# A hybrid decoder block on one core: the input projection as seven products of halves

## The reference, cut to what matters

```
D_MODEL = 2048; SEQ = 512; N_META = 16
POOL_WIDTH = 1024; DN_WIDTH = 2048; DN_HEADS = 16; DN_HEAD_DIM = 128
IN_SPLIT_SIZES = (1024, 1024, 2048, 2048, 2048, 2048, 16, 16, 2048, 2048)

def hybrid_layer(h, ...):                       # h: (1, 528, 2048) float32
    xn = rmsnorm(h, norm_w)
    proj = xn @ w_in                            # (528, 2048) @ (2048, 14368)
    u_pool, z_pool, q, k, v, z_dn, b, a, gate_pool, gate_dn = split(proj)
    y_pool = causal_multiscale_pool(u_pool, pool_mix, pool_scale) * silu(z_pool)
    y_dn = gated_deltanet_branch(q, k, v, z_dn, b, a, ...)   # conv of 4 taps, silu,
                                                # chunked delta rule, 16 heads
    merged = sigmoid(gate_pool) * (y_pool @ w_pool_out) + sigmoid(gate_dn) * (y_dn @ w_dn_out)
    return h + merged @ w_o                     # then a final rmsnorm, meta tokens dropped
```

## Time and profile before

| | us |
|---|---|
| three runs | 1962.67, 1962.79, 1963.48 (median 1962.79) |
| span of the profiled execution | 1960.8 |
| PE busy | 1931.4 (99%) |
| PEld busy | 1724.3 (88%) |
| DVE busy | 921.4 (47%) |
| ACT busy | 726.0 (37%) |
| POOL busy | 78.3 (4%) |
| DMA, mean over the span | 115 GB/s |

### The profile page before, as it was taken

The page is one execution under the profiler, slowest core; times in us unless marked ns, Lnnn a source line. Parts: engine busy times, 40 slices in busy tenths (PEclk is TensorE's granted clock), DMA queues, the critical chain, the costliest instruction groups (busy, mean ns, idle before and its releaser), DMA issues.

```text
span 1960.8 us, 35753 instructions
## 1 busy us (share of the span) xinstructions
PE 1931.4 (99%) x13729; PEld 1724.3 (88%) x13729; DVE 921.4 (47%) x2315; ACT 726.0 (37%) x2136; POOL 78.3 (4%) x105
## 2 busy tenths in 40 slices
PE   5999999999999999999999999999999999999998
PEld 5888899999999999999999988888888888888886
DVE  6333343656556466555646654322224444335332
ACT  5422223435353443535345353323234322224232
POOL 4000000000000000000000000000000000000000
PEclk8999999999999999999999999999999999999999
DMA  6133342433333242333334144333443534347302
GB/s 222 59 103 102 102 134 88 119 95 86 95 120 90 87 124 69 96 111 100 91 107 123 44 131 127 119 107 128 134 162 134 186 118 139 118 139 279 108 22 86
DMA packets 221302, 225.73 MB, mean 115 GB/s; under 512 B 33665, under 2 KB 197978, under 8 KB 220522
## 3 DMA queue, kind: packets, MB, share of 16 engines
q1 hardware_dynamic: 158898, 180.17, 28.1%
q10 hardware_dynamic: 55944, 22.63, 4.6%
q0 software_dynamic: 6336, 21.08, 3.4%
HBM read 199.65 MB, written 25.30 MB: 115 GB/s over the span
## 4 chain that ended last, share of the span: by engine, by line
PE 97%; ACT 1%; DVE 1%; issue 0%; POOL 0%; DMA 0%; ACTq 0%; SPq 0%; DVEq 0%
PE pj L530 82%; PE pg L530 10%; PE pt L530 3%; PE pt L679 1%; PE pg L781 0%; POOL xl L1696 0%; DVE fst L1233 0%; ACT xsquare L908 0%; DMA xt<-in_meta_tokens 0%; PE pj L574 0%; DVE xl L1239 0%; ACT wh L868 0%; DVE xt L1246 0%; ACT L1041 0%; ACT L1070 0%
## 5 line engine op out<-in xcount | busy, mean ns | idle before, releaser
L530 PE MATMUL pj<-xh,wh 128*128 128x512 f32 (+3 forms) x2688 | 735.1, 328 | 3.2 <-DVE wl L1208 3.1
L530 PE MATMUL pj<-xh,wl 128*128 128x512 f32 (+3 forms) x2688 | 712.4, 319 | 0.0
L530 PE MATMUL pj<-xl,wh 128*128 128x512 f32 (+3 forms) x2688 | 712.3, 319 | 0.0
L1208 DVE TENSOR_TENSOR wl<-raw,wh 128x256 fp32r<-128x256 f32 x896 | 344.2, 421 | 603.0 <-ACT wh L868 601.5
L530 PEld LDWEIGHTS pj<-xh,wh 128*128 128x128 f32 x2688 | 446.9, 189 | 43.2 <-DVE wl L1208 3.4
L530 PEld LDWEIGHTS pj<-xh,wl 128*128 128x128 f32 x2688 | 448.4, 188 | 35.9
L530 PEld LDWEIGHTS pj<-xl,wh 128*128 128x128 f32 x2688 | 448.8, 189 | 33.9 <-issue 1.0
L868 ACT ACTIVATE wh<-raw 128x256 fp32r<-128x256 f32 x896 | 307.0, 410 | 64.7 <-issue 45.0
L868 ACT ACTIVATE wh<-rawb 128x256 fp32r<-128x256 f32 (+1 forms) x224 | 85.0, 437 | 217.0 <-PE pj L530 189.8
L530 PE MATMUL pj<-yl,wh 128*128 128x512 f32 x384 | 149.5, 389 | 0.0
L530 PE MATMUL pj<-yh,wl 128*128 128x512 f32 x384 | 149.5, 389 | 0.0
(11 more groups left out here) (243 smaller groups left out, 1784.3 us busy)
## 6 DMA issues: line engine op xcount, KB each, us to landing
raw<-in_w_in SPq DMA_DIRECT2D x112, 1024.0 KB, 6.2
rawb<-in_w_dn_out SPq DMA_DIRECT2D x16, 1024.0 KB, 6.3
rawb<-in_w_o SPq DMA_DIRECT2D x12, 1024.0 KB, 5.3
gates_scratch<-stg ACTq DMA_DIRECT2D x32, 256.0 KB, 2.1
rawb<-in_w_pool_out SPq DMA_DIRECT2D x8, 1024.0 KB, 5.7
gst<-gates_scratch POOLq DMA_DIRECT2D x32, 256.0 KB, 3.1
yraw<-branch_scratch SPq DMA_DIRECT2D x1, 5632.0 KB, 23.1
xt<-in_x SPq DMA_DIRECT2D x4, 1024.0 KB, 6.2
```

Of the source, the lines that this page charges most:

```text
L530: return pe.matmul(dst, lhs, rhs, start=start, stop=stop)
L1208: tt(wl[:, j, 2 * q:2 * q + 2, :], raw[:, 2 * par + h, 2 * q:2 * q + 2, c * P:(c + 1) * P], wh[:, j, 2 * q:2 * q + 2, :].bitcast(F32), ALU ...
```

## The change

The 256 columns and 2048 rows of a block are taken as four quarters of 1024 rows by 128 columns, A and C (upper rows), B and F (lower rows), and the positions as two halves of 264 (eight meta tokens and 256 positions each). The four half-size results are got from seven products instead of eight, each of 1024 rows by 128 columns by one half of positions: sums and differences of quarters and of input halves go in, and sums of products come out. A product is two chunks of four weight tiles. The order in a block is `(1, 4, 6, 2, 5, NEXT, 3)`, where NEXT is product 7 of the following block.

- PE: 7 x 8 x 3 = 168 matmuls of 264 columns a block (q: 260; z, z_pool and gate: 256) in place of 96 of 512 or 192 of 256 to 272. Products 4, 6, 5, NEXT and 3 wait for a copy or an addition of the block.
- ACT: 14 high-part copies of 512 elements instead of 16 of 256, and three copies of a bank into `snap` a block; one of the four results is copied out by `last_to_time` or squashed in two parts.
- DVE: 14 subtractions of 512 elements instead of 16 of 256; four weight sums of 1024 elements (`s1` to `s4`); three combinations of a bank with a snapshot (`c11`, `c21`, `c22`).
- SP: one transfer of 1 MB for A and C together with 1 KB runs, and one of 512 KB with 512 B runs for each of B and F, into five quarter buffers that are written over in place; SP's loads are written out in an order of their own, with the reloads of k, q, v and z among them.
- The weight buffers hold four chunks (`RINGS`), split three chunks ahead of PE (`AHEAD`).
- To make room, k, q, v and z of a pair go through a scratch tensor in HBM (`head_scratch`): ACT stores each head after its SiLU, SP reloads them one pair later. `zst` and `vch` now lie in `tm`, so POOL waits for the store of a pair before it loads the row sums of the next.
- At the start the five input combinations and their parts are made (ten halves of 1056 elements each for sums and for low parts, most on DVE), some before the first product and some within block 0. The small product for beta and decay moves from pool group 0 to group 1.
- The delta steps are spread over 112 half-chunk hooks (`delta_step`), with step m at hook 15m/8.

```diff
+NEXT = 0
+ORDER_FIRST = (1, 2, 7, 6, 4, 5, NEXT, 3)
+ORDER = (1, 4, 6, 2, 5, NEXT, 3)
+ORDER_LAST = (1, 4, 6, 2, 5, 3)
+AHEAD = 3
+RINGS = 4
...
+            def block_loads(b, col, between=None):
+
+                order, base = order_of(b), base_of(b)
+                sp.wait_ge(lo_done, base + after(order, 1))
+                sp.wait_ge(sum_done, 4 * b + 3)
+                load_ac(col)
+                if between == "v":
+                    load_vch(between_pair[0])
+                sp.wait_ge(lo_done, base + after(order, 5))
+                load_raw(RF, col)
+                if between == "kq":
+                    load_kq(between_pair[0])
+                if between == "z":
+                    load_zst(between_pair[0])
+                sp.wait_ge(lo_done, base + after(order, 3))
+                load_raw(RB, col)
...
+        def delta_step(h):
+
+            return next((m for m in range(O0 + 6) if 15 * m // 8 == h), None)
...
-                    for w, xx, first, last in ((wh, xh, True, False), (wh, xl, False, False), (wl, xh, False, True)):
-                        for dst, c0, n in halves:
-                            mm = product(dst, w[:, slot, k, :], xx[:, kt, c0:c0 + n],
-                                         first and kt == 0, last and kt == KT - 1)
...
+                for i, what in enumerate(order):
+                    if what == 1:
+                        need(pe, last_done, b - 1)
+                    elif what == 2:
+                        need(pe, add_done, 3 * b)
+                    elif what == 4:
+                        pe.wait_ge(snap_done, snapped(b, "s4"))
+                    elif what == 6:
+                        pe.wait_ge(snap_done, snapped(b, "s1"))
+                    elif what == 5:
+                        pe.wait_ge(snap_done, snapped(b, "s2"))
+                    elif what == 3:
+                        pe.wait_ge(add_done, added(b, "C22"))
+                    elif what == NEXT:
+                        pe.wait_ge(add_done, added(b, "C21"))
...
+                        pe.wait_ge(lo_done, base + chunk + 1)
+                        for k in range(HK):
+                            kt = HK * h + k
+                            for w, xx, one, last in ((wh, xh, True, False), (wh, xl, False, False), (wl, xh, False, True)):
+                                mm = pe.matmul(bank[:, c0:TH], w[:, slot, k, :], xx[what][:, kt, c0:TH],
+                                               start=opens and one and kt == 0, stop=closes and last and kt == KH - 1,
+                                               skip_group_check=True)
...
+                of, what, half, chunk, slot = split_target(b, par, t)
+                dve.wait_ge(hi_done, chunk + 1)
+                tt(wl[:, slot, :, :], weights(SLOT_OF[what])[:, HK * half:HK * (half + 1), :], wh[:, slot, :, :].bitcast(F32),
+                   ALU.subtract).then_inc(lo_done, 1)
...
+                for t in range(2 * len(order)):
+                    if t == (3 if first else 0):
+                        s2(b)
+                    if t == (7 if first else 1):
+                        s1(b)
+                    if t == (8 if first else 5):
+                        s4(b)
+                    if not last and t == (9 if first else 6):
+                        s3(b + 1)
+                    split_lo(b, par, t)
+                    if t == (10 if first else 7):
+                        free(1)
+                        c21(b, kind, dst[1])
+                    if t == (12 if first else 10):
+                        c22(b, par, kind, dst[1])
+                    event(t)
+                    if t == (13 if kind in ("k", "q", "v") or first else 12 if kind == "u" else 11):
+                        free(0)
+                        c11(b, kind, dst[0])
+                    hook(2 * t)
+                    hook(2 * t + 1)
...
+            row_differences(0)
+            with pool.Fori(1, PAIRS) as d:
+                head_out(d - 1)
+                pool.wait_ge(y_stored, 16 * d)
+                row_differences(d)
+            head_out(PAIRS - 1)
```

More of the change, by code:

```diff
@@ L74, with base_of, order_of, after @@
 NGATE = 2 * D // CW
-CB = 512
-NCB = D // CB
 NCP = CP_GATE0 + NGATE
+SLOT_OF = {1: 0, 2: 2, 3: 2, 4: 3, 5: 3, 6: 4, 7: 4, NEXT: 4}
+RA, RC, RB, RF, RE = range(5)
+def base_of(b):
+    return 0 if isinstance(b, int) and b == 0 else 14 * b + 2
+ALL_CHUNKS = base_of(NCP - 1) + 2 * len(ORDER_LAST)
+def order_of(b):
+    if isinstance(b, int):
+        return ORDER_FIRST if b == 0 else ORDER_LAST if b == NCP - 1 else ORDER
+    return ORDER
+def after(order, product):
+    return 2 * order.index(product) + 2
 CI = 0
@@ new lines, in gate_block, with event, last_pair, before @@
+            def gate_block(i, par, before, hook):
+                def event(t):
+                    before(t)
+                    ends = 2 * len(order_of(CP_GATE0 + i))
+                    if t == ends - 2:
+                        second_squashed(CP_GATE0 + i, stg[:, 1, :], ACT.Sigmoid, gate_sig)
+                    if t == ends - 1:
+                        gate_store(i, 1)
+                block_acts(CP_GATE0 + i, par, "gate", "gate", event, hook)
+            for k in range(4):
+                def last_pair(h, k=k):
+                    m = delta_step(28 * k + h)
+                    if m is not None:
+                        delta(PAIRS - 1, m)
+                def before(t, k=k):
+                    if k == 0:
+                        z_tail(PAIRS - 1, t)
+                    else:
+                        gate_tail(k - 1, 1 - k % 2, t)
+                gate_block(k, k % 2, before, last_pair)
@@ new lines, in block_steps @@
+            def block_steps(b, par, kind, dst, free, event, hook):
+                order = order_of(b)
+                first, last = 7 in order, NEXT not in order
+                for t in range(2 * len(order)):
+                    if t == (3 if first else 0):
[12 more added lines that the diff above has]
+                        c22(b, par, kind, dst[1])
+                    event(t)
+                    if t == (13 if kind in ("k", "q", "v") or first else 12 if kind == "u" else 11):
+                        free(0)
+                        c11(b, kind, dst[0])
+                    hook(2 * t)
+                    hook(2 * t + 1)
@@ new lines, in x_lo_part @@
+            def x_lo_part(what, half, source, high):
+                rows = slice(HK * half, HK * (half + 1))
+                dve.wait_ge(x_hi, high)
+                tt(xl[what][:, rows, :], source[:, rows, :], xh[what][:, rows, :].bitcast(F32), ALU.subtract).then_inc(x_lo, 1)
+            dve.wait_ge(x_f, 17)
+            for half in range(2):
+                x_total(fd, f12, f22, ALU.subtract, half)
+            split_lo(0, 0, -3)
+            s3(0)
+            split_lo(0, 0, -2)
+            for half in range(2):
+                x_lo_part(7, half, fd, 5 + half)
+                dve.wait_ge(x_sum, 1 + half)
+                dve.wait_ge(x_lo, 1 + half)
+                x_total(fd, fd, f11, ALU.subtract, half)
@@ new lines, in free, with hook @@
+                    def free(c, k=k):
+                        if k == 3:
+                            dve.wait_ge(head_stored[c], 16 * (4 * p + 3))
+                        else:
+                            need(dve, conv_step, (6 * p + 2 * k + 1 - c) * 4)
+                    def hook(h, k=k):
+                        m = delta_step(28 * k + h)
+                        if d is not None and m is not None:
+                            delta(d, m)
+                    dst = [xin[:, TAPS - 1:]] * 2 if k < 3 else [stg[:, c, :] for c in range(2)]
```

1045 lines of the change are left out of this document (652 added, 393 removed).

## The result

The changed kernel takes 2038.18 us (median of four runs, 2030.75 to 2041.82), the kernel before 1962.75: a ratio of 1.038, 95% interval 1.036 to 1.040. Predicted were 1890 us and a gain of 73; it came out 75 us slower, on the side to which I had given 0.08. The profiled execution has a span of 2035.1 us.

A forecast was written before the change was run, and what follows sets the result against it. PE bound the kernel before; after, DVE in k and q, PE in v and z. Gains 12 (pool stage), 10 (pair 0), 19 (seven pairs), 7 and 25 (gate blocks) make 73: 1962.8 - 73, about 1890 us, range 1842 to 1932.

The forecast's parts named there:

- PE's part: Projection matmuls: a u, k or v block wins 3.1 us, q 2.8, the others 2.2; a pair wins 11.2.
- DVE's part: DVE's work per block goes from 5.4 to 14.1 us; a pair has 102.7 us of DVE against 104.7 of PE.
- the sum by blocks: In a pair, the larger of DVE and PE per block: k 27.4, q 25.6, v 34.5, z 20.5, together 108 us.
- Waits that the change adds: In a pair, waits between engines and for `dec`: 4 us for k and q, 1 for v, making 113 us.
- the clock: PE's clock should stay at 1.00 (2.4 GHz); if waits push it lower, the forecast is too low; no size given.
- The chain for `dec`: On POOL: y's store, row sums, then `dec`, 13.9 us in all; DVE waits 1.5 us for it in block k.
- The start: Block 0 ends near 67 us, with 36 us of DVE work from about 31 us on; it loses 6 us.
- The end: Passage from the gate blocks to stage B: 1 us taken off the 26.4 us won by twelve gate blocks.
- the fourth: Rival: delta-step rounds between PE and DVE cost twice the waits, P 128.7, 2000 us, deciding from P = 123.4; chance 0.08.
- P: Length of a pair with a delta rule: 115.7 us before, forecast 113, forecast's own range 109 to 117.
- The formula: Whole kernel's time as 1962.8 - 54 - 7 x (115.7 - P), with P the length of a pair.

The follow-up runs named there:

- e5: e4 with the row sums loaded into `dec` itself before y is stored, and v's reload waiting for that store: 1973.7 us.
- e4: Changed kernel with the pair loop written out, k and q reloaded eight chunks earlier, and the `yraw` load cut into five pieces: 1987.2 us.
- e1: Changed kernel with the loop over pairs 1 to 7 written out on PE, ACT and DVE: 2032.6 us.
- e6: e5 with the loop over the pairs kept on PE, ACT and DVE: 2015.0 us.
- e3: Changed kernel with the 5 MB `yraw` load cut into five pieces issued between earlier weight loads: 2023.9 us.
- e7: e5 with DVE's four weight sums cut to an eighth in every block but the first, output not the reference's: 1909.1 us.
- e12: e5 with 12 and 5 filler matmuls on PE ahead of two waits in the inverse of block v: 1971.1 us.
- e11: e5 with nine of the fourteen steps of the block inverse left out on DVE, output not the reference's: 1949.6 us.
- e8: e5 with the two rounds that turn and square q moved ahead of the block inverse: 1995.5 us.

## Why the prediction was wrong

**PE's part** was right where nothing interferes. The gate stores come every 19.88 us, so a matmul of 256 columns starts every 118.3 ns instead of the 117 taken; the timeline of the changed kernel, gate blocks 6 to 8:

```profile
1391.83 0.37 ACT L1091 ACTIVATE stg<-pj 128x256 f32<-128x256 f32 x1
1411.71 0.37 ACT L1091 ACTIVATE stg<-pj 128x256 f32<-128x256 f32 x1
1431.59 0.37 ACT L1091 ACTIVATE stg<-pj 128x256 f32<-128x256 f32 x1
```

The gain there, 1.9 us a block, is real; besides it only pair 0, without a delta rule, gained (91.0 to 82.1 us). In the pairs PE's part was somewhat too low: it is busy 35.9 of v's 37.4 us in pair 4 of e5 and 21.9 of z's 22.9 in pair 7 of e4, both at a clock of 1.00, where I had 34.5 and 20.5.

**DVE's part** was right: 102.1 us a pair against 102.7, and with the waits for the loop and for `dec` taken away (e5) k and q took 27.5 and 29.2 us, 56.7 together, where the sum by blocks with 4 us of waits for the two had 57.

**"Waits that the change adds" is the step that failed.** I charged 5 us a pair on top of 108; it was 16. Of the 11 between them, 3 are in k and q (60.1 us instead of 57) and 8 in v and z (64.1 instead of 56), where I had charged 1. Three terms are in it. First, the return to the head of the loop, which the sum didn't have at all: written out, z is 4.1 us shorter and q 2.4 (e1), 6.5 us a pair, and put back it costs 6.9 us a return (e6 against e5), clock included. It goes with the packets on q14, of which five fall at each return here and none in the kernel before (87 against 22 in all; 48 in e1, where nothing returns). The Trainium skill ("Runtime: NRT & Kernel Launch", "Instruction fetch mechanics") says that prefetch is sequential and a taken branch outside the window that is held makes the engine wait for its code. The trace agrees that there is a stop and that packets of code come with it, and that code written out has neither at this place; the price is from the runs alone, and what size a body may have, no run here shows. Second, v and z: with no stop left z still takes 22.9 us (e1, e4, and the last pair of the changed kernel) and v 36 at the least, against 20.5 and 34.5. About half is PE's own work (above) and half idle time of PE; where it comes from no run shows. Third, the clock: PE's stops bring the granted clock to 0.50 behind them. I had named this as what would make the forecast too low and gave it no price. In the profiled execution the deficit is 31 us in the pairs, 4 a pair, part of which is in the first term already, and 14 in the four gate blocks, where the third alone takes 45.4 us, against none in the pairs of the kernel before. The windows of that block in the changed kernel:

```profile
1264.30:1268.00 3.70, 2.11 (x119) 1.94 (x119) 2.34 (x8) 0.65 (x3) 0.00 (x0) 1.00 0.09 28
1268.00:1290.00 22.00, 22.00 (x187) 20.09 (x186) 10.04 (x19) 4.15 (x10) 0.00 (x0) 0.53 0.19 61
```

**The chain for `dec`** was put at 13.9 us and took 15.7: y's store landed after 7.6 us instead of 4.1 beside the reload of k and q, and the row sums were there after 5.2 us instead of 7.7. Its wait looked small in the changed kernel (8.4 us in all) and was 28 to 42 us once the stop was gone (e4, e1); taking it away gained 13.5 (e5).

**The start.** I gave DVE 36 us from 31 on and let the block end with them. The last part of the input did end at 30.0, but from 31 on DVE is busy 42.9 us and idle 4.8 (36.9 us of it after 37.00), since splits and a sum for the next block and the first steps of the pooling stand among the block's own work, and PE goes at a clock of 0.80. The windows of block 0 in the changed kernel:

```profile
0.00:37.00 37.00, 16.37 (x90) 14.62 (x91) 26.19 (x39) 21.87 (x27) 10.74 (x8) 0.90 0.61 193
37.00:78.70 41.70, 31.29 (x193) 30.33 (x193) 36.90 (x44) 18.24 (x29) 3.46 (x2) 0.80 0.20 57
```

12 us of the 22 lie here; the others, in the rest of the pool stage, were not taken apart by a run, but the trace has 6.7 us there in which PE waits for DVE's low parts.

**The end.** 1 us was charged for the passage and 20 were lost: 14 by the place of `yraw`'s load in SP's queue (e3), the rest by DVE, which has 21.7 us of work in a block of 17, and by the clock of 0.87. I had counted what each engine does in this block and not what SP issues behind its last weight load.

**The rivals.** By its number the fourth came true (P of 124.2, where it decides from 123.4), and by a part of its mechanism: less work on DVE shortens the pairs (e7). It had neither the return nor the clock, so that its number fits is luck in the main: with the loop written out and k and q reloaded earlier P is below 120 (e4). The formula with P = 124.2 gives 1968; the other 70 us are the start, the gate blocks beside the delta rule and the end, which I had all costed as averages.

No version that does all of the reference's work beats the kernel before: the best, e12, is 0.2 to 0.5% slower. The versions that do beat it, e7 and e11, both leave work of DVE out.

## What to carry to other kernels

Work moved from a full engine to an idle one is paid where the idle one is locally full: add it up for each stretch that the buffers between them can't even out, here for each block, and add the waits of the now full engine for the others, which no longer hide (in q, 25.5 us of work took 29). Two waits that end at the same place must be taken away together; an experiment that removes one and gains nothing hasn't cleared it. Look in the profile at whether a loop's head is reached without a stop, and write the loop out if it isn't.

## What the runs showed of the hardware

- The return of a 120 us loop, free in the kernel before, stopped PE, DVE and ACT for 4.1, 4.8 and 5.7 us in the mean (2.2, 2.9 and 3.3 in e6), with five packets on the instruction queue q14 around each return; the kernel before had none on it over six passes of its loop. Written out, the same instructions passed this place without the common stop.
- The granted clock of PE fell to the level of 1.2 GHz behind each of the six returns of the changed kernel, for 3 to 7 us, and behind stops of some 1.5 us among small matmuls, for 3 to 14 us in the pairs of e5 and for 20 in the third gate block of the changed kernel, there in some pairs and not in others. Runs of one kernel lay up to 22 us apart (e6, e8), those of the kernel before within 2.3.
- A POOL and a DVE instruction of 1024 elements that overlap took 2.31 and 2.27 us instead of 1.89 and 1.22.
- A store of 512 KB landed after 7.6 us beside a reload of 1 MB, and after some 4 without it.
